# Second block's mixer layers: when the decay rows, the channel transposes and the convolution stand in the queues

## What is computed

```python
for l in range(2):
    h = rmsnorm(x, norm_mix_g[l])
    uv, z, xbc, dt_raw, c_q, c_kv, k_rope = split_cols(h @ w_in[l])
    y_a = gmlp_mixer(uv, ...)      # gelu, rmsnorm of v, 128x128 causal mixing
    y_b = ssd_mixer(z, xbc, dt_raw, ...)
    y_c = mla_mixer(c_q, c_kv, k_rope, ...)
    x = x + concatenate([y_a, y_b, y_c]) @ w_out[l]
    x = x + squared_relu_mlp(rmsnorm(x, norm_mlp_g[l]), mlp_w1[l], mlp_w2[l])

def ssd_mixer(...):
    xbc = silu(causal_depthwise_conv(xbc, conv_w, conv_b))      # 4 taps, 640 channels
    xs, B, C = split(xbc)
    a = cumsum(dt * A)
    w = (C @ B.T) * exp(a[t] - a[s], causal) * dt[s]            # per head and chunk, 128x128
    y = w @ xs + exp(a) * (C @ state) + xs * d
    y = rmsnorm(y * silu(z), norm_g)
```

## Time and profile before

| | |
|---|---|
| runs of the kernel (3) | 1399.31, 1400.76, 1402.44 us; median 1400.76 |
| the profiled execution, time | 1398.37 us |
| its span | 1396.6 us |
| its mean granted clock of TensorE | 0.966 |
| TensorE busy / VectorE / ScalarE | 93% / 62% / 49% of the span |
| mixer layers | about 767 to 888 us and 1079 to 1199 us, each followed by an MLP |

### The profile page before, as it was taken

The page is one execution under the profiler, slowest core; times in us unless marked ns, Lnnn a source line. Parts: engine busy times, 40 slices in busy tenths (PEclk is TensorE's granted clock), DMA queues, the critical chain, the costliest instruction groups (busy, mean ns, idle before and its releaser), DMA issues. The chain is left out here.

```text
span 1396.6 us, 19837 instructions
## 1 busy us (share of the span) xinstructions
PE 1295.0 (93%) x7972; PEld 1130.7 (81%) x7972; DVE 870.4 (62%) x1511; ACT 687.4 (49%) x966; POOL 2.4 (0%) x8
## 2 busy tenths in 40 slices
PE   5998898989989999897998988999999987999997
PEld 5897787767878787786886986798998986899996
DVE  6546896567473756547447787665556877755545
ACT  4623477533356665474423656444433656443442
POOL 0000000000000000000000000000000000000000
PEclk9998999989999999998998999999999999999998
DMA  9325342534542434233223443365564443366561
GB/s 304 124 73 184 100 128 79 166 102 172 190 151 91 152 121 158 85 122 129 90 91 111 137 131 93 119 211 193 171 208 141 139 139 102 109 204 202 181 204 53
DMA packets 146914, 197.53 MB, mean 141 GB/s; under 512 B 4717, under 2 KB 102279, under 8 KB 146695
## 3 DMA queue, kind: packets, MB, share of 16 engines
q1 hardware_dynamic: 146694, 196.22, 43.9%
q0 software_dynamic: 128, 0.04, 0.0%
HBM read 195.20 MB, written 1.05 MB: 141 GB/s over the span
## 5 line engine op out<-in xcount | busy, mean ns | idle before, releaser
L1923 DVE TENSOR_TENSOR w_lo<-w_raw,w_hi 128x2048 fp32r<-128x2048 f32 (+5 forms) x190 | 413.4, 2183 | 166.1 <-ACT w_hi L1453 164.0
L1453 ACT ACTIVATE w_hi<-w_raw 128x2048 fp32r<-128x2048 f32 (+5 forms) x190 | 345.7, 1828 | 299.6 <-PE bank L455 285.8
L453 PE MATMUL bank<-h_hi,w_hi 128*128 128x256 f32 x976 | 282.3, 289 | 7.4 <-DVE w_lo L1923 3.7
L454 PE MATMUL bank<-h_lo,w_hi 128*128 128x256 f32 x976 | 278.6, 285 | 0.0
L455 PE MATMUL bank<-h_hi,w_lo 128*128 128x256 f32 x976 | 278.3, 285 | 0.0
L453 PE MATMUL bank<-w_hi,r_hi 128*128 128x512 f32 (+3 forms) x536 | 209.5, 391 | 7.6 <-DVE r_lo L2535 4.2
L454 PE MATMUL bank<-w_lo,r_hi 128*128 128x512 f32 (+3 forms) x536 | 205.7, 384 | 0.0
L455 PE MATMUL bank<-w_hi,r_lo 128*128 128x512 f32 (+3 forms) x536 | 205.4, 383 | 0.0
L453 PEld LDWEIGHTS bank<-h_hi,w_hi 128*128 128x128 f32 x976 | 189.8, 194 | 13.1 <-issue 5.2
L454 PEld LDWEIGHTS bank<-h_lo,w_hi 128*128 128x128 f32 x976 | 189.9, 195 | 0.6
L455 PEld LDWEIGHTS bank<-h_hi,w_lo 128*128 128x128 f32 x976 | 189.7, 194 | 0.0
(11 more groups left out here) (262 smaller groups left out, 1376.8 us busy)
## 6 DMA issues: line engine op xcount, KB each, us to landing
w_raw<-in_mlp_w SPq DMA_DIRECT2D x64, 1024.0 KB, 5.4
w_raw<-in_w_out SPq DMA_DIRECT2D x24, 1024.0 KB, 5.1
w_raw<-in_w_in_c SPq DMA_DIRECT2D x48, 512.0 KB, 4.6
w_raw<-in_w_in_c SPq DMA_DIRECT2D x18, 1024.0 KB, 5.1
w_raw<-in_w_in_a SPq DMA_DIRECT2D x12, 1024.0 KB, 5.9
w_raw<-in_w_in_b SPq DMA_DIRECT2D x12, 1024.0 KB, 5.2
w_raw<-in_w_in SPq DMA_DIRECT2D x8, 1024.0 KB, 5.3
w_raw<-in_w_out SPq DMA_DIRECT2D x8, 512.0 KB, 3.8
```

Of the source, the lines that this page charges most:

```text
L453: nc.tensor.matmul(o, lhs[0], rhs[0], start=start, stop=False)
L454: nc.tensor.matmul(o, lhs[0], rhs[1], start=False, stop=False)
L1453: nc.scalar.activation(w_hi[:, u % SPLIT_SLOTS, 0:kts * n], w_raw[:, u % RAW_SLOTS, 0:kts * n], ACT.Copy).then_inc(w_rounded.sem, w_rounde ...
L1923: v.tensor_tensor(w_lo[:, s, 0:m], w_raw[:, u % RAW_SLOTS, 0:m], w_hi[:, s, 0:m].bitcast(F32), ALU.subtract)\
```

## The change

It touches only the mixer layers of the second block, on all three engines.

1. The decay rows are written in three banks of four heads each, and stand after the first half of the `z` projection instead of ahead of `keys_values`.
2. The `z` projection is split in its two units. Between the second unit's two row blocks stand the channel transposes and `inputs_outputs`. The second half of `uv` moves ahead of `turn_heads(0)`. The bank tables change with it.
3. On VectorE all three `scale_channels` stand ahead of the convolution; `decay_exponents` stands behind it; `rope_key` moves up to before the key latents; `rope_queries` and `build_keys` move down, behind `state_rows`; `chunk_weights` goes ahead of `spatial_weights`.
4. ScalarE writes the no-rope part of the keys straight to `ktok` (two instructions of 128x3x64 for each bank instead of one of 128x384), so that VectorE's two copies L2456 go. Its exponentials of the decay stand behind the silu of the convolution, the silu of the first `z` block and the evacuation of `xs`. The squares of the SSD output stand ahead of the first gelu, and `head_tiles(0)` behind the second.

```diff
-        CUM_BANK, QB_BANK, RC_BANK, KV_BANK, Z_BANK = 7, (3, 4, 5, 0), (1, 2, 6, 7), (3, 4, 5, 0), (1, 2)
-        XS_BANK, CB_BANK, WST_BANK, UV_BANK, ST_BANK, YD_BANK, YO_BANK = (6, 7), 3, 0, (4, 5), 6, (7, 1), 2
-        QT_BANK, KT_BANK, GATING_BANK, MIXER_BANK, HEAD_BANK, MLA_TURN_BANK = (0, 3, 0), (6, 7, 6), 1, (2, 3), (3, 6), (6, 7)
+        CUM_BANK, QB_BANK, RC_BANK, KV_BANK, Z_BANK = 7, (3, 4, 5, 0), (1, 2, 6), (3, 4, 5, 0), (7, 3)
+        XS_BANK, CB_BANK, WST_BANK, UV_BANK, ST_BANK, YD_BANK, YO_BANK = (4, 5), 0, 6, (1, 2), 4, (5, 0), 4
+        QT_BANK, KT_BANK, GATING_BANK, MIXER_BANK, HEAD_BANK, MLA_TURN_BANK = (7, 6, 7), (3, 0, 3), 0, (1, 2), (3, 6), (6, 7)
...
                 queries()
+                keys_values()
...
+                proj_half("z", Z_BANK, C_Z, SSD_W, 0)
                 decay_rows()
-                keys_values()
-                proj("z", Z_BANK, C_Z, SSD_W)
+                proj_half("z", Z_BANK, C_Z, SSD_W, 1, (0,))
                 turn_channels()
                 inputs_outputs()
+                proj_half("z", Z_BANK, C_Z, SSD_W, 1, (1,))
                 spatial_weights()
...
                 from_state()
+                proj_half("uv", UV_BANK, C_UV, UV, 1)
                 turn_heads(0)
-                proj_half("uv", UV_BANK, C_UV, UV, 1)
                 turn_heads(1)
...
+                rope_key()
                 latent(1, "ck", ckt, 0, KV_RANK)
                 scale_channels(0, 2)
                 latents_lo(0)
                 latents_lo(1)
                 weights((L, "xbc", 0), 3)
-                convolve(0, (0, 1))
                 scale_channels(1, 2)
                 latents_lo(2)
+                scale_channels(2, 1)
                 weights((L, "xbc", 1), 3)
                 cumulated()
+                convolve(0, (0, 1))
+                weights((L, "kv", 1, 1), 1)
                 convolve(1, (2, 3))
-                scale_channels(2, 1)
-                weights((L, "kv", 1, 1), 1)
+                weights((L, "kv", 1, 1), 2)
+                convolve(2, (4,))
                 decay_exponents()
-                convolve(2, (4,))
-                weights((L, "kv", 1, 1), 2)
-                rope_key()
+                weights((L, "z", 0), 1)
+                chunk_inputs()
+                skip_rows()
+                chunk_weights()
+                weights((L, "z", 1), 2)
+                spatial_weights()
+                state_rows()
                 rope_queries()
                 build_keys()
-                weights((L, "z", 1), 1)
-                chunk_inputs()
...
```

More of the change, by code:

```diff
@@ L1139, in decay_rows @@
                 def decay_rows():
[L1140 to L1147, removed]
+                    for q in range(3):
+                        o = taken(RC_BANK[q], dve_read, (L, "rc", q))
+                        for h in range(4):
+                            at = 64 + 4 * q + h
+                            i = nc.tensor.matmul(o[:, h * P:(h + 1) * P], stat[:, at:at + 1].to_broadcast([P, P]), K("upto"),
+                                                 start=True, stop=True)
+                        i.then_inc(product_done.sem, product_done.next((L, "rc", q)))
                 def queries():
@@ L1315, in _ @@
                 queries()
+                keys_values()
+                for key in (("z", 0), ("xs", 0), ("xs", 1)):
+                    act_read.at((L, *key))
+                proj_half("z", Z_BANK, C_Z, SSD_W, 0)
                 decay_rows()
-                keys_values()
-                proj("z", Z_BANK, C_Z, SSD_W)
+                proj_half("z", Z_BANK, C_Z, SSD_W, 1, (0,))
                 turn_channels()
                 inputs_outputs()
+                proj_half("z", Z_BANK, C_Z, SSD_W, 1, (1,))
                 spatial_weights()
-                for key in ("st", ("qt", 0), ("kt", 0)):
-                    act_read.at((L, key) if key == "st" else (L, *key))
+                act_read.at((L, "st"))
                 for h in range(M_H):
@@ L1836, in _ @@
                 for c in range(NB):
+                    act.wait_ge(dve_read.sem, dve_read.at((L, "rc", c + 1)))
                     for g in range(2):
-                        act.wait_ge(dve_read.sem, dve_read.at((L, "rc", c, g)))
                         d3 = decay[:, c * SSD_H + 3 * g:c * SSD_H + 3 * g + 3, :]
                         nc.scalar.activation(d3, d3, ACT.Exp).then_inc(exp_seg.sem, exp_seg.next((L, c, g)))
[L1841 to L1851, removed]
+                half_chunk_read("z", 1, zg[:, 1, :], bank[Z_BANK[1]][:, 0:SSD_W], ACT.Silu, S_(9, 1))
                 evac((L, "st"), st_sb, bank[ST_BANK][:, 0:192])
[L1853 to L1856, removed]
                 act.wait_ge(z_gated.sem, z_gated.at(L))
@@ L1859, in _ @@
                     row_squares(split_t[:, 1, 0:192], flat2(y_b)[:, 192 * g:192 * g + 192], S_(496 + g, 1), (L, "y", g))
-                half_chunk_read("uv", 1, uv[:, 1, :], bank[UV_BANK[1]][:, :], ACT.Gelu_apprx_tanh, S_(9, 1))
-                act.wait_ge(act_read.sem, act_read.at((L, "uv", 1)))
-                row_squares(split_t[:, 1, 0:256], uv[:, 1, 256:512], S_(49, 1), (L, "uv", 1))
+                for b in range(NB):
+                    half_chunk_read("uv", b, uv[:, b, :], bank[UV_BANK[b]][:, :], ACT.Gelu_apprx_tanh, S_(8 + b, 1))
+                    if b == 1:
+                        head_tiles(0)
+                    act.wait_ge(act_read.sem, act_read.at((L, "uv", b)))
+                    row_squares(split_t[:, 1, 0:256], uv[:, b, 256:512], S_(48 + b, 1), (L, "uv", b))
                 head_tiles(1)
@@ L2372, in rope_key @@
                 def rope_key():
+                    for b in range(NB):
+                        dve.wait_ge(act_read.sem, act_read.at((L, "ck", b)))
                     tt(kr3, ku, cos_m, MUL)
@@ L2422, in decay_exponents @@
                 def decay_exponents():
[L2423 to L2430, removed]
+                    for q in range(3):
+                        product((L, "rc", q), 1)
+                        for h in range(4):
+                            i = 4 * q + h
+                            ins = v.scalar_tensor_tensor(decay[:, i, :], bank[RC_BANK[q]][:, h * P:(h + 1) * P], cum[:, i:i + 1],
+                                                         K("future_st"), SUB, ADD)
+                        ins.then_inc(dve_read.sem, dve_read.next((L, "rc", q)))
                 def rope_queries():
```

37 lines of the change are left out of this document (28 added, 9 removed).

## The result

| | before | after |
|---|---|---|
| runs | 1396.85 to 1402.44 us (4) | 1380.73 to 1386.20 us (4) |
| median | 1400.03 us | 1385.03 us |
| ratio, 95% interval | | 0.9889 [0.9859, 0.9919] |
| profiled execution | 1398.37 us | 1385.87 us |

Of that us, 0.7 come from the kernel before, whose median is 1400.03 in these four runs and was 1400.76 in the three that the prediction started from. The page of the changed kernel answers to the earlier trace rows: TensorE is busy for 7.7 us less with the same number of instructions (by windows, 228.56 us before and 219.69 after in the two mixer layers), which already says that part of the gain isn't waiting but clock.

A forecast was written before the change was run, and what follows sets the result against it. TensorE's list was taken as the path from 809 to 827 us, then ScalarE and VectorE from 841 to the scores. Layer gains 5.7 + 5.4 = 11.1 us off 1400.76 gave 1389.7 us, range 1386 to 1397.

The forecast's parts named there:

- The gap and its cause: Decay matmuls: TensorE waits 3.85 us (second mixer layer's gap 4.34) for the last channel tile's scaling, queued behind convolution.
- TensorE up to the transposes: First mixer layer, queries to channel transposes: TensorE's summed list reaches the transposes at 818.2 us; start put at 818.4, 8.5 earlier.
- The convolution's end: VectorE, first mixer layer: the last convolution ends at 815.5 us instead of 816.5.
- The others keep up: After the transposes: ScalarE and VectorE have chunk weights ready at 828.0, wanted at 829.3; both new table loads hidden.
- the margin of 1.3 us for the chunk weights: VectorE ahead of within_chunks: weights ready at 828.0 us, TensorE wants them at 829.3.
- From there to the scores: Gated product to scores: ScalarE's 8.5 us chain decides; spatial_norm at 844.1, 6.0 earlier; layers gain 5.7 and 5.4 us.
- move as a block: Spatial mixing, output projection and MLP keep their order and simply shift by the layer gains, 5.7 and 5.4 us.
- more than forecast: Rival: the slow clock at 860 us vanishes too, winning 1.6 us more per layer, 1386.5 us; chance 0.04.
- the low clock moves forward: Rival: a 2.7 us wait behind turn_heads(1) drops the clock before spatial mixing; gain 2.8 per layer, 1395 us; chance 0.10.
- The dearer table loads: Rival: ScalarE's table loads cost more than their trace row, 2.6 us per layer unhidden, 1395 us; chance 0.05.
- Loss behind the product: Rival: after 842 us the path depends on something unmoved, such as a weight unit's load; 1400 us; chance 0.06.
- a late load: Rival "slower": the load for uv's second unit delays ScalarE; 10 us late in both layers gives 1407 us; chance 0.05.

The follow-up runs named there:

- the scaling with the clock held: Kernel before with all scale_channels ahead of the convolutions on VectorE, plus 21 idle matmuls per mixer layer on TensorE: 1386.57 us, ratio 0.9893.
- the old order: Changed kernel with TensorE, ScalarE and VectorE in their previous order from behind from_state on: 1392.59 us, ratio 0.9941.
- the shorter chain: Changed kernel with gelu's table fetched in ScalarE's wait, head_tiles(0) and a rounding behind the second gelu, one VectorE w_lo ahead of state_rows: 1384.39 us.
- the two added loads: Changed kernel with a one-element gelu and silu ahead of the small exponential, so two more ScalarE table loads per layer: 1385.29 us, ratio 0.9888.
- the early decay rows: Changed kernel with decay_rows back ahead of keys_values, but in three banks: 1384.70 us, ratio 0.9896.

## Why the prediction was right in its cause and short in its size

- *The gap and its cause*: right. Scaled early, the last channel tile no longer holds bank 2, and the scaling with the clock held (1386.57 us, 13.9 less than before) is nearly the whole gain. It was worth less than thought without the clock: 5.2 us, not 9 or more.
- *TensorE up to the transposes*, forecast 818.4: 820.84 - 2.73 = 818.1. *The convolution's end*, forecast 815.5: 816.54 + 1.53 - 2.73 = 815.3. The prediction had TensorE's and ScalarE's sides meet at 818.2. They don't: the silu's load is not on the path, and the silu is done at 819.38 - 2.73 = 816.7, 1.4 ahead of the transposes. TensorE's list alone decides.
- *The others keep up*: right, but the margin of 1.3 us for the chunk weights was too small: with ScalarE's exponentials 3 us later nothing waited. The weights are made one head at a time (12 operations in 3.2 us), and TensorE needs the first of them first.
- *From there to the scores*: right. The spatial norm at 843.7 (846.41 - 2.73; forecast 844.1), the second pair at 847.6 (forecast 848.5), so 6.4 and 5.6 us instead of 5.7 and 5.4.
- *The failed step* is the term of the sum that let everything behind the scores "move as a block", with the low clock of 860 to 863 us in it. It vanished in both layers: from the output projection to the value products 7.64 us in both, before 9.21 and 8.93. That is 2.9 us, and the steps ahead of it gave 0.95 more than forecast; with about 0.5 further behind, it makes 15.4 us by the layers against 11.1. It stood among the rivals, as "more than forecast", with a chance of 0.04 and a price of 1.6 us per layer (measured 1.57 and 1.29): right as a price, wrong as a chance. Its 1386.5 was itself 1.5 us too high, 0.7 by the median of the kernel before and the rest by the small surpluses.
- *The rival "the low clock moves forward"* is a real mechanism of this code, and took half of the gain where the scaling was hoisted alone; in the changed kernel it didn't occur. The argument against it was that the old gaps had left the clock at 0.99 to 860. That does not carry over to another set of gaps.
- *The dearer table loads* fell: the forecast by the row held. The prediction prices this rival twice, at about 1393 and at 1395; by its own 2.6 us per layer it is 1395. By the Trainium skill, ScalarE: Activation LUTs, section "What ACT_TABLE_LOAD costs", two more loads in a layer would by an estimate from its figures (2 x 2.66) take 5.3 us of ScalarE. The rows above show 3.0 with the two added operations in it, and the measurement decides.
- *Loss behind the product* and *a late load* did not occur: TensorE has no wait from 805 to 841 us that is worth naming (36.89 of 37.00 us busy to 842).

## What to carry to other kernels

Where an engine's trace has a low clock anywhere near the change, price each stretch at both clocks and give both cases a real chance: here holding it was worth 3.3 to 9.1 us by the medians of four pairs of kernels (3.0 to 8.8 by the layers), as much as the waits themselves. When an edit shortens the path and the time hardly moves, put idle matmuls in TensorE's waits before giving the edit up: it tells clock from waiting in one run, and may be kept. Compare layers from their own first instruction, since an untouched part of the program can shift by 4 us.

## What the hardware did that was not expected

- TensorE's clock fell to the 1.2 GHz level (granted 0.50) behind waits of 1.3 to 2.9 us, none of them longer, in both layers of the kernel before and of those with the early scaling alone, the old order, the shorter chain and the two added loads. From the decay rows to the value products it stayed full in both layers of the changed kernel in two profiles, and with the early decay rows. (At the MLP's first unit it is low before and after: 0.51 from 894 to 896 us before, 0.55 from 889 to 891 after.) With the 21 or 26 idle matmuls it was full behind those waits each time: 10 layers of five kernels, of which the changed kernel's two had it full without them.
- What decides it between such patterns stays open. The kernel with two more loads has the same TensorE list as the changed one and the same wait (2.77 and 2.76 us), and its clock fell right behind that one wait, which followed 20 us of matmuls without any wait worth naming (19.88 of the 20.00 us from 817.71); only ScalarE and VectorE differ 20 us earlier. The kernel with the shorter chain waits less than the changed one (2.38, 1.31 and 1.50 us; 2.76, 1.28, 1.31 and 1.50 there) and lost its clock too. So it is not settled that the new order of the change is what protects its clock, only that the old order lost it.
- A table load can lie in the wait of the operation that needs it: the silu's load ran at 814.53, while ScalarE was waiting for the convolution until 818.10. Before, it started at 821.20 and the silu followed at 822.49; that it would move ahead of the wait was not foreseen, though the prediction had seen the gelu's load in a wait. It is not so for every load: before, the one ahead of the scores' exponential (853.65 us) started only after 0.84 us of waiting for the scores' maximum.
